# Growing the transposed triangle inverses in all four quadrants of the matmul array at once, with the second half added across partitions

## The reference, cut to what matters

```
def step(state, inp):
    r_t, w_t, k_t, v_t, a_t, b_t = inp
    sa = jnp.einsum('bhij,bhj->bhi', state, a_t)
    state = state * w_t[:, :, None, :] + sa[..., None] * b_t[:, :, None, :] + v_t[..., None] * k_t[:, :, None, :]
    return state, jnp.einsum('bhij,bhj->bhi', state, r_t)
```

## The kernel before, in words

**What runs between.** The order of each engine's work is written out by hand, and each engine runs its list in order. The attention units i = 0 to 7 are woven between the levels. On VectorE:

```
        scores(3)
        grown(2)
        weighted(3)

        scores(4)
        compressed_turned(1)
        grown(3)
        weighted(4)

        scores(5)
        grown(4)
        weighted(5)
```

## Time and profile before

| what | value |
|---|---|
| runs | 1322.5, 1320.2, 1321.83 us |
| median | 1321.83 us |
| the profiled execution's own time | 1320.47 us |
| its span, first to last instruction | 1318.7 us |
| mean granted TensorE clock | 0.971 |
| TensorE matmul, VectorE, ScalarE busy, share of the span | 93%, 30%, 21% |

### The profile page before, as it was taken

How to read it: one execution, slowest core, us unless ns; L and a number is a source line. 1 busy time by engine, 2 the same in 40 slices (tenths; PEclk the granted TensorE clock), 3 DMA queues, 4 the chain that set the end, 5 groups by cost and what they waited for, 6 DMA issues and landing times.

```text
span 1318.7 us, 20861 instructions
## 1 busy us (share of the span) xinstructions
PE 1220.1 (93%) x8776; PEld 673.4 (51%) x8776; DVE 400.1 (30%) x1016; ACT 271.0 (21%) x558; POOL 40.7 (3%) x34
## 2 busy tenths in 40 slices
PE   9999999999999888798999999999999997787987
PEld 4777755444443333443588887454444443333433
DVE  1287856121112111111247655152121112101111
ACT  1343523111010000000233656031101110000102
POOL 1003200000000000000000111000000000000000
PEclk9999999999999989798999999999999999887989
DMA  7633289999999999999944474979999999999996
GB/s 270 209 104 161 85 344 392 428 427 425 428 427 426 427 427 428 424 426 425 359 163 176 160 287 166 408 274 426 425 428 429 426 425 429 427 427 424 426 428 266
DMA packets 55898, 463.62 MB, mean 352 GB/s; under 512 B 8624, under 2 KB 9936, under 8 KB 26608
## 3 DMA queue, kind: packets, MB, share of 16 engines
q1 hardware_dynamic: 55792, 462.16, 85.3%
HBM read 461.06 MB, written 1.08 MB: 350 GB/s over the span
## 4 chain that ended last, share of the span: by engine, by line
PE 64%; DMA 26%; DVE 4%; issue 2%; ACT 2%; SPq 1%; another core or an unknown queue 1%; DVEq 0%; ACTq 0%
DMA raw<-in_moe_w_up 18%; PE bank L2262 9%; DMA raw<-in_moe_w_gate 7%; PE bank L2243 6%; PE bank L2923 5%; PE sums L2309 5%; PE bank L2199 5%; PE sums L2923 4%; PE bank L3055 4%; PE bank L2300 4%; PE bank L2287 3%; PE bank L1264 3%; PE bank L1296 2%; PE bank L2273 2%; SPq L332 1%
## 5 line engine op out<-in xcount | busy, mean ns | idle before, releaser
L2262 PE MATMUL bank<-raw,xg 128*32 128x512 f32 x1664 | 232.6, 647 | 50.9 <-DMA raw<-in_moe_w_up 44.9
L2172 DVE TENSOR_TENSOR aT<-bank,sg 128x128 f32<-128x128 f32 (+1 forms) x64 | 20.2, 316 | 550.6 <-ACT sg L2067 550.6
L2262 PEld LDWEIGHTS bank<-raw,xg 128*32 128x32 f32 x1664 | 59.0, 118 | 199.3 <-issue 117.6
L2199 PE MATMUL bank<-sel,ux 128*128 128x64 f32 (+1 forms) x896 | 117.7, 288 | 13.3 <-DVE sel L2089 12.4
L2199 PEld LDWEIGHTS bank<-sel,ux 128*128 128x128 f32 x896 | 110.9, 202 | 37.0 <-issue 21.6
L2309 PE MATMUL sums<-ys,selT 64*128 64x512 f32 x512 | 127.2, 615 | 1.6 <-DVE ys L2185 1.6
L2064 ACT COPY gus<-bank 128x512 f32<-128x512 f32 x64 | 37.5, 585 | 440.0 <-PE bank L2262 334.9
L2300 PE MATMUL bank<-raw,aT 128*32 128x512 f32 x832 | 100.1, 598 | 9.4 <-DVE aT L2172 9.4
L2309 PEld LDWEIGHTS sums<-ys,selT 64*128 64x128 f32 x512 | 44.2, 186 | 84.1 <-issue 80.0
L2243 PE MATMUL bank<-raw,xg 128*64 128x512 f32 x384 | 84.7, 594 | 0.0
L2923 PE MATMUL bank<-uT,wr 128*128 128x256 f32 x352 | 78.2, 381 | 0.0
(11 more groups left out here) (438 smaller groups left out, 1236.6 us busy)
## 6 DMA issues: line engine op xcount, KB each, us to landing
raw<-in_moe_w_gate SPq DMA_DIRECT2D x54, 2048.0 KB, 40.7
raw<-in_moe_w_up SPq DMA_DIRECT2D x54, 2048.0 KB, 45.2
raw<-in_moe_w_down SPq DMA_DIRECT2D x54, 2048.0 KB, 45.1
raw<-in_moe_w_gate SPq DMA_DIRECT2D x20, 1024.0 KB, 11.4
raw<-in_moe_w_up SPq DMA_DIRECT2D x20, 1024.0 KB, 10.7
raw<-in_moe_w_down SPq DMA_DIRECT2D x20, 1024.0 KB, 10.1
wr<-in_ssm_w_in SPq DMA_DIRECT2D x10, 2048.0 KB, 8.5
odd<-in_hyb_w_in SPq DMA_DIRECT2D x2, 2048.0 KB, 10.3
```

The costliest lines, as they stand in the source:

```text
L2199: i = T.matmul(bank[SIDE_BANK][:, k * n:(k + 1) * n].rearrange("p (x s) -> p x s", x=2), ux[:, t, 4 * half + k, :], src[:, t, :, :], start ...
L2262: i = T.matmul(bank[GU_BANK][CAP_S * c:CAP_S * c + CAP_S, :], xg_f[:, x, 4 * half + k, :], raw[:, slot, k * FH:(k + 1) * FH], start=(half ...
```

## The change

The transposed growth is made like the plain one: both g in one call of `squares`, matmuls alternating, results written to half q rather than to the half of `triT`, with one signal for both. For g = 1 the results then lie on the other partition half than the tile that they are added to, so that addition is made in two instructions, each of 64 partitions, which read one half of the bank and add into the other half of the tile.

```
@@ VectorE, grown(l)
-                    go(V.tensor_tensor(sl, bank_of(name, l, g)[:, :].rearrange("p (c s) -> p c s", s=CHK), sl,
-                                       ALU.add), "read", name, l, g)
+                    grew = bank_of(name, l, g)[:, :].rearrange("p (c s) -> p c s", s=CHK)
+                    if name == "dTT" and g:
+                        for q in range(2):
+                            go(V.tensor_tensor(sl[at64(1 - q)], grew[at64(q)], sl[at64(1 - q)], ALU.add),
+                               *(("read", name, l, g) if q else ()))
+                    else:
+                        go(V.tensor_tensor(sl, grew, sl, ALU.add), "read", name, l, g)
@@ TensorE, grown(l)
-            for g in range(2):
-                squares({g: take(pe, "dTT", l, g, pool=right)}, prod, triT, crossed, crossed).then_inc(
-                    pe_done, PE.one(("dTT", l, g)))
+            bs = {g: take(pe, "dTT", l, g, pool=right) for g in range(2)}
+            squares(bs, prod, triT, crossed, straight).then_inc(pe_done, PE.one(("dTT", l, 1)))
+            new[("dTT", l, 0)] = new[("dTT", l, 1)]
```

## The result

The changed kernel takes 1327.0 us (median of six runs, 1325.83 to 1329.13) beside 1322.6 for the kernel before (six runs, 1320.2 to 1326.53): a ratio of 1.0035, 95% interval 1.0022 to 1.0048. It is slower by 4.4 us, where the prediction said +1.8 and no change that can be told. The profiled execution of after is a long one (1329.13 us), that of before a short one (1320.47), so the two traces differ by 8.7 us, twice what the medians do; part of why single runs differ so much comes out of the experiments.

What follows compares the result with a forecast made beforehand. In the changed stage TensorE's products and VectorE's list compete, and delay at `wu` counts in full. Terms 0 + 0.66 + 0.20 + 0.14 + 0.82 + 0 = +1.8 us on 1321.83 gave 1323.6 us, range 1320.6 to 1326.0.

Steps and rivals of the forecast that it cites:

- rival C: Transposed growth: four pairs of halves at once run no faster than two; sum 5.3 us, 1327.1 us; chance 0.03.
- d: Extra VectorE time a level from three `dTT` additions in place of two, up to the normalisation: taken as 0.82 us.
- B: VectorE: a half addition costs more than a full one; at 0.3 us more each, +4.2, 1326.0 us; chance 0.12.
- A: Second product of level 1: the instruction stall moves with TensorE, keeping 0.88 us; sum +0.9, 1322.7 us; chance 0.21.
- D: TensorE sets the pace throughout and all five savings count: 4.4 us less, 1317.4 us; chance 0.04.
- The list's sum: Delays of `wu` by VectorE's extra additions, summed over the five levels: +1.8 us.
- levels 3 and 4: Delays added up to the turn of unit 5: 0.20 at TensorE, 0.14 in VectorE's part, then 0.82 us.
- level 5: The third addition fits barely before the normalisation, which waits for ScalarE's exponentials: 0 added.
- Level by level: Step following TensorE's and VectorE's timelines through the five levels to `wu`, which moves from 161.62 to about 163.4 us.
- Level 2: Normalisation of unit 3 ends at 138.39 instead of 137.57, so TensorE's turn comes 0.66 us later.
- Level 1: TensorE's 0.88 us saving is swallowed by a stall on a late instruction block, ending at 128.08 as before: 0.
- What it saves it spends waiting: At level 2 TensorE spends its saving waiting for VectorE's normalisation of unit 3; the turn is +0.66 us.

Runs made afterwards that it cites:

- split only: Kernel before with only the second addition of the transposed growth cut into two halves, without crossing and without the new growth: 1324.24 us, ratio 1.0014.
- the split: Kernel before with that addition cut in two, plus two projection loads earlier, the last load later and GpSimd's additions behind two normalisations: 1320.46 us, ratio 0.9985.
- early loads: Two of SP's four output-weight loads issued ahead of the levels: 1318.29 us in the kernel before, 1332.6 us in the changed kernel.
- GpSimd's waits: Changed kernel with GpSimd's bias addition and last masking made to wait for the normalisations of units 2 and 3: 1327.84 us; with early loads 1323.43 us.
- second profile of after: The changed kernel run and profiled again without any edit, against the kernel before: 1329.47 us, ratio 1.0055.
- masking later: Changed kernel with GpSimd's last masking, for level 4, made to wait for the normalisation of unit 3: 1326.71 us, ratio 1.0028.
- reordered list: Changed kernel with early loads and GpSimd's waits, its `dTT` additions of levels 1, 3 and 4 moved later in VectorE's list: 1325.37 us, ratio 1.0024.
- after cleared: Changed kernel with early loads, the last load behind product 5, and GpSimd's additions behind the normalisations of units 2 and 3: 1322.03 us, ratio 1.0002.
- before reordered: Kernel before with early loads and the `dTT` additions of levels 1, 3 and 4 moved later in VectorE's list: 1322.14 us, ratio 1.0003.
- levels 2 to 5: The change made at levels 2 to 5, with level 1 as in the kernel before: 1330.94 us, ratio 1.0052.
- early loads and waits: Changed kernel with two output-weight loads ahead of the levels and GpSimd waiting for the normalisations of units 2 and 3: 1323.43 us, ratio 1.0009.
- level 1 only: The change made at level 1 alone, with levels 2 to 5 as in the kernel before: 1324.17 us, ratio 1.0014.

## Why the prediction was wrong

**What it had right.** Four quadrants at once take 1.11 to 1.16 us, so rival C is out; that its price, 1327.1, is nearly the measured time is chance. A half addition over the crossing costs what a full one costs: d is 0.79, and two halves take 1.41 us with the crossing (after) and without (split only), so B is out, though the time landed beyond B's. The end of the first stall is set by the burst and moves with it, and `wu` did not come earlier with TensorE; A and D are out. TensorE's saving is worth nothing. The list's sum, 1.8, is what the split costs when all else is cleared away, and levels 3 and 4 of the trace of after agree with it within 0.1; level 5, put at 0, took 0.2 to 0.4. And what is late at `wu` is late at the end.

**The step that failed is "Level by level", where it let each delay be only its own size.** Behind the three additions it set the normalisation at its duration in before, and wherever TensorE spends its saving waiting it set that at nothing. Two things stood ready that it did not read, and a third it read only once:

- *GpSimd's list.* "Level 2" took 0.69 for the normalisation of unit 3, and "Level 1" said nothing of that of unit 2. Both lay beside GpSimd instructions of some 2.4 us with margins of 0.1 to 0.4 us, less than the 0.8 that they were pushed. The profile of before has those rows; no view of GpSimd was among those that the prediction read. Price: 2.04 us at unit 3 in the profile of after; up to 9.2 us, with the low clock behind it, where no stall hides it (early loads with and without GpSimd's waits).
- *The granted clock.* "What it saves it spends waiting" counts idle time as free. In the profile of after 10 us at the 1.2 GHz level follow, and the additions of level 2 are 3.78 late; in the cleared kernel `wu` takes 1.65 more.
- *The instruction blocks.* "Level 1" saw one block come late behind a burst, and took for free that TensorE then waits longer at it. It did not ask for the others. In before the block for the growth of level 3 arrives just ahead of the burst of the last load. In the second profile of after, and with the masking later, GpSimd's waits and the reordered list, it arrives 2.8 to 3.4 us after that load's issue and stalls TensorE for 1.2 to 2.05 us; moved away, the load stalls nothing (after cleared). It is not that TensorE simply gets there sooner: counted from the first product of level 1, before reaches that growth after 22.96 us, the second profile of after, 25.01. In these profiles what decides is whether the block or the load's data comes first.

These stand in for each other, which is why taking away one alone gained little (masking later 1326.71, GpSimd's waits 1327.84, against 1327.0 and 1329.47 for the change in its two sets), and would make single runs of it spread, as they do over 7 us: its two profiles paid different ones. Cleared of the collisions and of the bursts, the change costs 1322.03 - 1318.68 = 3.4 us: 1.8 the list, 1.6 by medians for the faster growth, where the one pair of profiles (after and split) shows 1.65 of low clock and 0.42 of a later start. The rest of the 4.4 to 7.9 us seen in the two sets is collision, stalls and low clock, and I did not settle its division: it differs from execution to execution.

**What stays open.** What exactly makes the clock fall. Before rode out a stall of 2.15 us at 1.00 in the profile shown, and before reordered a wait of 2.44; the split fell with a stall of 1.98. `wu` lasted 3.3 to 3.6 us in the first profile of after, with levels 2 to 5, with the masking later, with early loads and waits, and in after cleared, but 1.98 in the second profile of after, with level 1 only and in four other variants of after. So whether `wu` pays the 1.65 is a matter of the execution, and how often it does in after cleared I can't say from one profile; idle time of TensorE stands ahead of every fall, but no run gave a size of it that decides.

## What to carry to other kernels

An instruction added to an engine that runs its list in order is priced not only by its duration but by what the next instructions then meet: look in the trace at what runs on GpSimd and in the DMA queues within that distance, and how wide the gap is through which they now slip. Work taken from an engine that then waits is not merely worth nothing: it can bring that engine earlier to a late instruction block, as in level 1, or leave it idle, and idle stretches stood ahead of every fall of its clock here. When parts of a change don't add up, clear the disturbances in both kernels alike and compare again; here one of those clearings, the two early loads, made the kernel before 3.3 us faster, without the change.

## What the runs showed of the hardware

A VectorE instruction of 128 by 4 elements lasted up to 2.24 us when it met a GpSimd instruction of some 2.35, and 0.17 alone. From one round of matmuls of 64 by 64 to the next it took some 58 ns, whether the round filled two quadrants or four. Cutting an addition of 128 by 512 into two halves of 64 partitions cost 0.8 us, with the crossing or without. Bursts of loads held blocks of TensorE's instructions and cost 1.2 to 3.1 us at a time; moving two loads removed one such stall and 3.3 us of the time. After idle stretches of TensorE its granted clock stood at 0.50 for some 3 to 10 us within an otherwise busy stage, and matmul groups took 1.7 to 1.9 times as long.
